# Moving the second attention's half steps, eighth by eighth, in between the column groups of the second block's projections

## The chip, the cores and the metric

The kernel runs on one core of one Trainium2 chip. The metric is the time of one execution on the device in microseconds (us); lower is better. The engines are named as the profile names them: PE is TensorE (PEld its weight loads), DVE is VectorE, ACT is ScalarE, POOL is GpSimd and SP is SyncE, which here only issues transfers.

## The reference: what is computed

512 tokens (x is 512 x 1024, float32) pass through two transformer blocks. The change touches the first half of the second block alone:

```python
h = rms_norm(x, norm_mix[l])
proj = h @ w_in[l]                       # 1024 x 2048
q, k, v, u = jnp.split(proj, [512, 1024, 1536], axis=-1)
a = moba_attention(q, k, v)              # 8 heads of 64
p = multiscale_pool(u, w_pool[l], pool_scale[l])
x = x + jnp.concatenate([a, p], axis=-1) @ w_out[l]
h = rms_norm(x, norm_mlp[l])
x = x + jnp.square(jax.nn.relu(h @ w_up[l])) @ w_down[l]
```

With 512 tokens and blocks of 256, every query attends to all tokens before it: `moba_attention` is causal softmax attention with an added bias of minus slope times distance, one slope for each head. `multiscale_pool` takes, for four groups of 128 channels of u, the mean over the last 2, 4, 8 or 16 tokens, subtracts the token, multiplies by a 128 x 128 matrix and scales each channel. The first block (its own attention beside a recurrence called rwkv7, then a feed-forward part) comes before it and is not changed.

## The kernel before

Everything is float32. Each large product is made of three products of rounded parts: an operand x is kept as `x_hi` (x rounded by a copy) and `x_lo` (x minus x_hi), and hi times hi, hi times lo and lo times hi are added up in PSUM. The 512 tokens are four row tiles (TT = 4) of 128 (P); the 1024 channels are eight tiles (KT = 8). Weights come in **groups** of 1024 x 256 (1 MB), numbered G_... through the whole program: SP loads group g into `w_raw[g % 2]`, ACT copies it to `w_hi[g % 2]` (`split` on ACT), DVE subtracts to get `w_lo[g % 2]` (`split` on DVE), and PE uses it. A group takes PE 48 matmuls of 512 columns or 96 of 256, and gives two PSUM tiles (T_... counts them; `mm_done` counts them finished, `tile_evacuated` counts them copied out; banks 0 to 3 rotate).

Every engine has its own program, written out by hand in order; engines wait for each other only through counted semaphores, and an engine does its instructions in the order of its text. So the order in the text is what sets the order of the work. The second block's mixing half stands thus on PE:

```python
first_tiles(N_MIX2, G_U2, T_U2)          # u: groups 49, 50
product_loop(G_QK2, T_QK2, 2)            # q, k: groups 51 to 54, channels on partitions (L404 to L406)
product_natural(G_V2, T_V2)              # v: groups 55, 56, tokens on partitions (L430 to L432)
```

then four small products of the pooled groups with `wpool` (L966, float32), then `attention(1)`, then the output product (L439 to L441) of groups 57 and 58 in `natural_group`, and of 59 and 60 in `out_pair`. Groups 61 and on are the feed-forward part.

`attention(b)` loops over four pairs of heads. A **half step** is one head and one tile of 128 queries, so there are 32. It is a chain over three engines: PE makes the scores (L912, of `qs` and the keys `ks0`, `ks1`, in which POOL has zeroed the other head's 64 channels, so that each product runs over 128 rows); DVE adds the bias (L1857) and takes the maximum (L1860, as a minimum of the negated scores); ACT takes the exponential with its sum (L1339); PE transposes (L919); ACT copies the transposes out (L1345); PE multiplies by the values (L928); DVE divides (L1844, L1846). After the four pairs PE transposes the result (L951), ACT and DVE make its hi and lo parts (L1350, L1425), and only then the output product can begin.

The first block's attention is built in another way: its half steps stand between steps of the recurrence, its scores (L779) use the 64 rows of the head alone, and bias and maximum are one DVE instruction (L1749) that writes over what it is to hold, with the exponential (L1257) in place. Its transposes are L788, the copies L1266, the products with the values L798.

DVE also makes the pooling windows (L1916 to L1924): before the first of them it takes the reciprocal of `rcnt` (L1911), 4 x 512 counts on each partition, which POOL has built (L2160, L2163).

## Time and profile before

| what | value |
|---|---|
| time before, median of 3 runs | 1400.87 us (1399.13 to 1403.6) |
| the profiled execution's own time | 1397.37 us |
| span of its trace | 1395.7 us |
| mean granted clock of TensorE | 0.982 |
| PE busy | 1304.2 us, 93% of the span |
| DVE busy | 635.5 us, 46% |
| ACT busy | 470.3 us, 34% |
| POOL busy | 250.8 us, 18% |

The profile is of one execution. An engine's busy time is the sum of its instructions; matmuls are pipelined and their ends are modelled, so the distance between the starts of two matmuls says more than the length of one. PEclk is the share of TensorE's full clock that was granted. The time outside the span is 1397.37 - 1395.7 = 1.7 us.

### The profile page before, as it was taken

How to read it: one execution, taken by the hardware profiler on the slowest of the kernel's cores; microseconds unless marked ns; L12 is line 12 of the kernel's file. 1: busy time of each engine (PE TensorE's matmuls, PEld its weight loads, DVE VectorE, ACT ScalarE, POOL GpSimd, SP SyncE). 2: the span in 40 equal slices, each digit the busy share in tenths (PEclk: the TensorE clock that was granted, in tenths of full speed). 3: DMA queues.
4: the chain of work that ended last, by engine and by line, in shares of the span. 5: the costliest groups of instructions: out<-in, count | busy, mean ns of one | idle time of the engine just before them, and what ended most of it. 6: DMA issues, size and time to landing. Idle time of an engine off the chain costs nothing.

```text
span 1395.7 us, 25137 instructions
## 1 busy us (share of the span) xinstructions
PE 1304.2 (93%) x10577; PEld 1163.4 (83%) x10577; DVE 635.5 (46%) x763; ACT 470.3 (34%) x758; POOL 250.8 (18%) x228
## 2 busy tenths in 40 slices
PE   5999989888799999999999887987999999999998
PEld 5677878777699889988899876865998899988998
DVE  5578635454347552134422646265255432245323
ACT  4446435335245222222222431266232211222222
POOL 6013325232102220012211030110003200022000
PEclk9999999999899999999999998998999999999999
DMA  5223100001052322223242122100313322222321
GB/s 181 75 61 120 61 2 3 2 3 50 14 182 75 107 91 95 90 91 104 72 151 92 61 68 91 61 1 19 118 61 104 106 91 91 90 90 90 106 92 61
DMA packets 99929, 108.95 MB, mean 78 GB/s; under 512 B 1907, under 2 KB 97189, under 8 KB 99845
## 3 DMA queue, kind: packets, MB, share of 16 engines
q1 hardware_dynamic: 99764, 107.45, 23.9%
q8 instruction: 67, 1.10, 0.3%
q0 software_dynamic: 80, 0.26, 0.1%
q14 instruction: 18, 0.14, 0.0%
HBM read 105.60 MB, written 2.10 MB: 77 GB/s over the span
## 4 chain that ended last, share of the span: by engine, by line
PE 78%; DVE 9%; issue 5%; ACT 4%; POOL 2%; DVEq 2%; POOLq 1%; ACTq 0%; DMA 0%
PE ps L404 11%; PE ps L406 11%; PE ps L405 11%; PE ps L439 10%; PE ps L440 10%; PE ps L441 10%; DVE w_lo L1420 2%; PE ps L490 1%; PE ps L491 1%; PE ps L492 1%; PE ps L432 1%; PE ps L430 1%; PE ps L431 1%; DVE rcnt L1911 1%; PE ps L668 1%
## 5 line engine op out<-in xcount | busy, mean ns | idle before, releaser
L1420 DVE TENSOR_TENSOR w_lo<-w_raw,w_hi 128x2048 fp32r<-128x2048 f32 (+1 forms) x93 | 212.1, 2280 | 241.4 <-ACT w_hi L985 238.2
L439 PE MATMUL ps<-w_hi,a_hi 128*128 128x256 f32 x1024 | 288.4, 282 | 0.9 <-DVE w_lo L1420 0.9
L440 PE MATMUL ps<-w_lo,a_hi 128*128 128x256 f32 x1024 | 288.0, 281 | 0.0
L441 PE MATMUL ps<-w_hi,a_lo 128*128 128x256 f32 x1024 | 288.0, 281 | 0.0
L404 PE MATMUL ps<-h_hi,w_hi 128*128 128x512 f32 x672 | 270.9, 403 | 13.1 <-DVE w_lo L1420 12.8
L406 PE MATMUL ps<-h_hi,w_lo 128*128 128x512 f32 x672 | 266.1, 396 | 0.0
L405 PE MATMUL ps<-h_lo,w_hi 128*128 128x512 f32 x672 | 266.0, 396 | 0.0
L985 ACT ACTIVATE w_hi<-w_raw 128x2048 fp32r<-128x2048 f32 (+1 forms) x90 | 171.2, 1903 | 162.8 <-PE ps L441 141.1
L2141 POOL TENSOR_TENSOR hsq<-tmp 128x512 f32<-128x512 f32 x64 | 103.3, 1616 | 568.3 <-ACT tmp L989 568.3
L439 PEld LDWEIGHTS ps<-w_hi,a_hi 128*128 128x128 f32 x1024 | 193.2, 189 | 1.5 <-DVE w_lo L1420 1.3
L440 PEld LDWEIGHTS ps<-w_lo,a_hi 128*128 128x128 f32 x1024 | 193.2, 189 | 0.2
L441 PEld LDWEIGHTS ps<-w_hi,a_lo 128*128 128x128 f32 x1024 | 193.2, 189 | 0.0
L404 PEld LDWEIGHTS ps<-h_hi,w_hi 128*128 128x128 f32 x672 | 126.5, 188 | 47.2 <-issue 14.8
L405 PEld LDWEIGHTS ps<-h_lo,w_hi 128*128 128x128 f32 x672 | 126.6, 188 | 32.4 <-issue 2.4
L406 PEld LDWEIGHTS ps<-h_hi,w_lo 128*128 128x128 f32 x672 | 126.4, 188 | 30.8
L1517 DVE TENSOR_TENSOR a_hi<-tmp 128x512 f32 (+1 forms) x64 | 47.5, 745 | 169.7 <-ACT tmp L989 169.7
L989 ACT ACTIVATE tmp<-ps 128x512 f32<-128x512 f32 x64 | 38.2, 598 | 248.8 <-PE ps L406 229.0
L439 PE MATMUL ps<-w_hi,h_hi 128*128 128x256 f32 x256 | 74.9, 292 | 11.3 <-DVE h_lo L1425 10.9
L490 PE MATMUL ps<-h_hi,w_hi 128*128 128x256 f32 x224 | 65.6, 293 | 12.2 <-DVE h_lo L1442 8.7
L440 PE MATMUL ps<-w_lo,h_hi 128*128 128x256 f32 x256 | 73.7, 288 | 0.0
L441 PE MATMUL ps<-w_hi,h_lo 128*128 128x256 f32 x256 | 73.6, 287 | 0.0
L491 PE MATMUL ps<-h_lo,w_hi 128*128 128x256 f32 x224 | 64.4, 288 | 0.0
(316 smaller groups left out, 1845.8 us busy)
## 6 DMA issues: line engine op xcount, KB each, us to landing
w_raw<-w_ffn_up_dram SPq DMA_DIRECT2D x16, 1024.0 KB, 5.3
w_raw<-w_ffn_down_dram SPq DMA_DIRECT2D x16, 1024.0 KB, 5.0
w_raw<-w_up_dram SPq DMA_DIRECT2D x16, 1024.0 KB, 5.3
w_raw<-w_down_dram SPq DMA_DIRECT2D x16, 1024.0 KB, 4.9
w_raw<-w_in_first_dram SPq DMA_DIRECT2D x12, 1024.0 KB, 5.3
w_raw<-w_out_dram SPq DMA_DIRECT2D x8, 1024.0 KB, 5.9
w_raw<-w_in_dram SPq DMA_DIRECT2D x8, 1024.0 KB, 5.3
xn<-x_dram SPq DMA_DIRECT2D x8, 512.0 KB, 6.5
```

Of the source, the lines that this page charges most:

```text
L404: mm(o, whi, hi[:, hb + k, :], start=first and k == 0, stop=False)
L405: mm(o, whi, lo[:, hb + k, :], start=False, stop=False)
L406: m = mm(o, wlo, hi[:, hb + k, :], start=False, stop=last and k == KT - 1)
L439: mm(o, hi[:, hb + k, tok], whi, start=first and own and k == ks[0], stop=False, skip_group_check=True)
L440: mm(o, hi[:, hb + k, tok], wlo, start=False, stop=False, skip_group_check=True)
L441: m = mm(o, lo[:, hb + k, tok], whi, start=False, stop=last and k == ks[-1], skip_group_check=True)
L490: mm(o[:, tok], whi, h_hi[:, k, tok], start=k == 0, stop=False)
L491: mm(o[:, tok], whi, h_lo[:, k, tok], start=False, stop=False)
L985: af(w_hi[:, g % 2, :, 0:n], w_raw[:, g % 2, :, 0:n], ACT.Copy).then_inc(sm["w_hi_ready"], 1)
L1420: v.tensor_tensor(w_lo[:, g % 2, :, 0:n], w_raw[:, g % 2, :, 0:n], w_hi[:, g % 2, :, 0:n].bitcast(F32), ALU.subtract).then_inc(sm["w_lo_re ...
L1517: v.tensor_tensor(a_hi[:, at_, :], tmp[:, m, :], tmp[:, m, :], ALU.mult)
L2141: g_.tensor_tensor(hsq[:, m % 2, :], tmp[:, m, :], tmp[:, m, :], ALU.mult)\
```

## The change

The second block's attention is rewritten after the manner of the first block's, and its half steps are put between eighths of the column groups. An eighth is an eighth of a group's matmuls: six of 512 columns or twelve of 256. After each comes a `tick`, and tick n holds the scores of half step n, the transposes of half step n - 2 and the products with the values of half step n - 3.

- **Order of the groups.** q and k of one pair of heads form one group (two transfers of 128 columns each), and the order is qk of pair 0, v of pairs 0 and 1, qk of pair 1, v of pairs 2 and 3, qk of pair 2, qk of pair 3 (`IN2`). Pairs 0, 1, 2 and 3 begin at ticks 0, 8, 24 and 32 (`PAIR_AT`); tick 0 is in the third group, ticks 32 to 47 are in the first two groups of the output product.
- **Attention.** Scores run over 64 rows; -1/8 is applied when q is copied out; POOL builds a table `bias` (eight multiplications of 128 x 512) in place of the staging of keys and queries; bias and minimum are one DVE instruction; `slopes`, `qs`, `ks0`, `ks1` go.
- **Pooling.** `rcnt` shrinks to 4 x 16 counts, the other tokens are multiplied by a constant; all four windows are made before DVE's third split; the small products stand after the first and the second group, and their results go to `m_hi` and `m_lo`.
- **Output product.** The groups are 512 rows by 512 columns (`mixed_step`): first the pooled rows, then the attention's. PE adds both into the same four PSUM tiles, DVE adds these to x at the end of the second group, and ACT then squares four pieces of 512 columns (before: eight of 256, four after each of the two groups).

The core of the diff:

```diff
-            product_loop(G_QK2, T_QK2, 2)
-            product_natural(G_V2, T_V2)
-            pe.wait_ge(sm["wpool_loaded"], 16)
-            for g in range(4):
...
-            attention(1)
-            pe.wait_ge(sm["hlo_ready"], H_OUT2 + 8)
-            for c in range(2):
-                natural_group(G_OUT2 + c, T_OUT2 + 2 * c, 0, h_hi, h_lo)
-            out_pair(N_FFN2, G_OUT2 + 2, T_OUT2 + 4)
+            in_and_attention()
+            last_pair(N_FFN2, G_OUT2 + 2, T_OUT2 + 4, mixed_rows)
```

```diff
+            def scores2(m):
+
+                p, t = m // 8, m // 2 % TT
+                pe.wait_ge(sm["max_ready"], 4 * H + m)
+                if m == 0:
+                    pe.wait_ge(sm["hlo_ready"], H_OUT2 + HP)
+                if t == 0:
+                    pe.wait_ge(sm["tile_evacuated"], T_IN2 + 2 * IN2.index(("qk", p)) + 2)
+                for e in range(2):
+                    mm(ps[:, 4 + e, 0:(t + 1) * P], qkT[half[e], p, t * P:(t + 1) * P], qkT[half[e], HP + p, 0:(t + 1) * P],
+                       start=True, stop=True).then_inc(sm["s_done"], 1)
...
+            def tick(n):
+
+                m = half_step(n)
+                if m is not None and m % 2 == 0:
+                    scores2(m)
+                m = half_step(n - 2)
+                if m is not None:
+                    turn_weights2(m)
+                m = half_step(n - 3)
+                if m is not None:
+                    values2(m)
+                if n in MIX_AT:
+                    turn_mix2(MIX_AT.index(n))
+
+            def pooled(g):
+
+                pe.wait_ge(sm["window_ready"], g + 1)
+                if g >= 2:
+                    pe.wait_ge(sm["hlo_ready"], H_OUT2 + g - 1)
...
+            def in_and_attention():
+
+                channels(0, None)
+                pe.wait_ge(sm["wpool_loaded"], 16)
+                pooled(0)
+                pooled(1)
+                tokens(1, None)
+                pooled(2)
+                pooled(3)
+                for n in range(2, 6):
+                    (channels if IN2[n][0] == "qk" else tokens)(n, 8 * (n - 2))
```

ACT's copies of the pooled products stand behind the copies of the second group (`mixed(1, j)`), and its last squares ahead of the split of group 60:

```diff
+            def in_and_attention():
+
+                split(G_IN2 + 1)
+                for j in range(2):
+                    mixed(0, j)
+                split(G_IN2 + 2)
+                for j in range(2):
+                    mixed(1, j)
+                for g in range(4):
+                    act.wait_ge(sm["pooled"], g + 1)
+                    af(m_hi[:, g, :], ps[:, 6 + g % 2, :], ACT.Copy, scale=cols("pool_scale_2", g)).then_inc(sm["hhi_ready"], 1)
...
+            in_and_attention()
+            act.wait_ge(sm["tile_evacuated"], T_OUT2 + 4)
+            for c in range(TT):
+                part(xn[:, c, 0:2 * GW], c, 0)
             split(G_OUT2 + 3)
```

POOL's table:

```diff
-            pool.wait_ge(sm["tile_evacuated"], T_V2)
-            clear_keys()
-            with pool.Fori(0, HP) as i:
-                stage_pair(i)
-                pool.wait_ge(sm["s_done"], at(8 * (HP + 1), i, 8))
+            for h in range(H):
+                m = g_.tensor_scalar(bias[:, h, :], delta[:, :], float(2.0 ** (-8.0 * (h + 1) / H)), None, ALU.mult)
+            m.then_inc(sm["bias_built"], 1)
```

How the instructions stand, read from the built programs. First PE, before, at the start of the second attention (L966 are the pooled products, `ks` the keys, `Pm` the exponentials, `PT` their transposes):

```order
L966 MATMUL ps<-uT,wpool 128x512 x4
L933 UNCONDITIONAL_BRANCH
L933 ISA
L912 MATMUL ps<-ks,qs 128x128
L912 MATMUL ps<-ks,qs 128x256
L912 MATMUL ps<-ks,qs 128x384
L917 ISA
L919 MATMUL ps<-ident,Pm 128x128
L912 MATMUL ps<-ks,qs 128x512
```

PE in the change, in the third group, from tick 1 to tick 3 (L1003 to L1005 are the projection; `tmp` now holds the exponentials and `hsq` their transposes):

```order
L1005 MATMUL ps<-h_hi,w_lo 128x512
L939 MATMUL ps<-qkT 128x256 x2
L948 MATMUL ps<-ident,tmp 128x128
L1003 MATMUL ps<-h_hi,w_hi 128x512
L1004 MATMUL ps<-h_lo,w_hi 128x512
L1005 MATMUL ps<-h_hi,w_lo 128x512
L1003 MATMUL ps<-h_hi,w_hi 128x512
L1004 MATMUL ps<-h_lo,w_hi 128x512
L1005 MATMUL ps<-h_hi,w_lo 128x512
L948 MATMUL ps<-ident,tmp 128x128
L959 MATMUL ps<-Vn,hsq 128x64
```

The attention's products, which stood together, now have six projection matmuls between one tick's and the next's.

DVE, in the change, behind the split of the second u group (L1567 is `split`, L2035 to L2046 are a window, `early` its first 16 tokens):

```order
L2091 RECIPROCAL rcnt<-rcnt 128x64
L2092 MEMSET upad 128x2x16
L2035 COPY upad<-uT 128x512
L2039 TENSOR_TENSOR upad<-upad 128x512
L2042 TENSOR_TENSOR early<-upad,rcnt 128x16
L2043 SCALAR_TENSOR_TENSOR uT<-upad,uT 128x496
L2046 TENSOR_TENSOR uT<-early,uT 128x16
L1567 TENSOR_TENSOR w_lo<-w_raw,w_hi 128x2048
L2035 COPY upad<-uT 128x512
L2039 TENSOR_TENSOR upad<-upad 128x512 x2
```

Before, the reciprocal was of 128x2048 and the split of group 52 stood right behind it, ahead of the first window; now the first window stands ahead of that split, and windows 1 to 3 ahead of the next.

ACT, in the change, at the end of the output product's second group (L1474 is the last hi part of the attention's result, L1104 the squares, L1095 `split`):

```order
L1474 ACTIVATE h_hi<-ps 128x512
L1104 ACTIVATE tmp,ssq<-xn 128x512
L1104 ACTIVATE hn_odd,ssq<-xn 128x512
L1104 ACTIVATE tmp,ssq<-xn 128x512
L1104 ACTIVATE hn_odd,ssq<-xn 128x512
L1095 ACTIVATE w_hi<-w_raw 128x2048
```

Before, only two squares of 128x256 stood between the last addition of that group and this split; now four of 128x512 do, and they wait for all four additions.

## Rows read from the trace of the kernel before

**Rows 1.** Windows: stretch, length, busy us of PE, PEld, DVE, ACT, POOL, PEclk, DMA.

```profile
821.70:833.00 11.30, 11.30 (x50) 8.86 (x48) 3.92 (x1) 3.00 (x3) 6.98 (x6) 1.00 0.31 93
833.00:844.40 11.40, 0.12 (x2) 0.03 (x1) 11.40 (x4) 2.40 (x2) 0.00 (x0) 0.69 0.00 0
844.40:902.20 57.80, 57.80 (x336) 50.87 (x337) 25.20 (x27) 12.61 (x13) 5.27 (x5) 0.97 0.29 91
902.20:907.00 4.80, 3.85 (x10) 1.18 (x8) 0.00 (x0) 3.54 (x6) 0.00 (x0) 1.00 0.00 0
907.00:963.40 56.40, 48.35 (x304) 36.82 (x304) 35.77 (x80) 37.07 (x100) 6.76 (x9) 1.00 0.00 0
...
973.30:998.00 24.70, 24.68 (x194) 24.68 (x195) 6.56 (x5) 5.59 (x14) 0.00 (x0) 0.92 0.47 150
```

**Rows 2.** Timeline of POOL, DVE and PE, 818 to 845: start, length, [idle before].

```profile
818.36 4.35 POOL L2160 CAST rcnt<-upad 128x512 f32<-128x512 int32 x4 [2.41 <-issue]
...
829.08 12.95 DVE L1911 RECIPROCAL rcnt<-rcnt 128x2048 f32<-128x2048 f32 x1 [7.96 <-POOL rcnt L2163]
...
844.37 0.79 PE L404 MATMUL ps<-h_hi,w_hi 128*128 128x512 f32 x1 [11.29 <-DVE w_lo L1420]
```

**Rows 3.** Timeline of PE inside the first block's attention.

```profile
188.78 0.49 PE L779 MATMUL ps<-qkT 64*128 64x128 f32 x4 [0.69 <-ACT Vn L1186]
189.21 0.56 PE L618 MATMUL ps<-krkv,bh 64*64 64x128 f32 x12
...
207.83 1.13 PE L779 MATMUL ps<-qkT 64*128 64x512 f32 x4
208.89 0.33 PE L788 MATMUL ps<-ident,Z 128*128 128x128 f32 x1
...
283.70 0.66 PE L788 MATMUL ps<-ident,Z 128*128 128x128 f32 x4
284.19 0.78 PE L798 MATMUL ps<-Vn,PT 128*128 128x64 f32 x6
284.90 0.28 PE L688 MATMUL ps<-hsq,Rm 64*64 64x64 f32 x2
```

**Rows 4.** Groups by line and form, 200 to 440: busy, mean ns | idle before.

```profile
L1257 ACT ACTIVATE Z<-Z,negmax 128x512 f32<-128x512 f32 x8 | 5.8, 724 | 7.4 <-DVE negmax L1749 7.4
L1749 DVE CUSTOM_DVE_ANT_0 Z<-lncount,ps 128x512 f32<-128x512 f32 x8 | 5.4, 672 | 2.0 <-PE ps L779 1.8 <-issue 0.2
```

**Rows 5.** Timeline of ACT at the end of the v groups.

```profile
902.41 0.60 ACT L1186 ACTIVATE Vn<-ps 128x512 f32<-128x512 f32 x1 [5.08 <-PE ps L432]
903.27 0.69 ACT L1389 ACTIVATE uT<-ps,par 128x512 f32<-128x512 f32 x1 [0.26 <-PE ps L966]
```

**Rows 6.** Timeline, POOL beside DVE in the second feed-forward part, and POOL's multiplications (L2163: ns min/median/max).

```profile
1047.99 2.89 POOL L2141 TENSOR_TENSOR hsq<-tmp 128x512 f32<-128x512 f32 x1 [1.36 <-ACT tmp L989]
...
1049.90 1.52 DVE L1517 TENSOR_TENSOR a_hi<-tmp 128x512 fp32r<-128x512 f32 x1
...
L2163 POOL TENSOR_SCALAR rcnt<-rcnt x4: 1481/1486/1517, 822.9 to 827.6; 128x512 f32<-128x512 f32 x4
```

**Rows 7.** Timeline around the split of group 60 and one square.

```profile
998.08 0.69 DVE L1530 TENSOR_TENSOR xn<-xn,ps 128x512 f32<-128x512 f32 x1 [4.75 <-PE ps L441]
...
999.87 1.90 ACT L985 ACTIVATE w_hi<-w_raw 128x2048 fp32r<-128x2048 f32 x1
...
1001.80 2.29 DVE L1420 TENSOR_TENSOR w_lo<-w_raw,w_hi 128x2048 fp32r<-128x2048 f32 x1 [3.03 <-ACT w_hi L985]
...
1004.15 0.39 PE L439 MATMUL ps<-w_hi,h_hi 128*128 128x256 f32 x1 [0.43 <-DVE w_lo L1420]
...
1022.00 0.63 ACT L994 ACTIVATE tmp<-xn 128x512 f32<-128x512 f32 x1 [3.24 <-DVE xn L1945]
```

**Rows 8.** A pause of PE and the window right behind it.

```profile
795.40 0.36 PE L490 MATMUL ps<-h_hi,w_hi 128*128 128x256 f32 x1 [3.40 <-DVE h_lo L1442]
...
795.40:799.40 4.00, 4.00 (x22) 4.00 (x23) 1.94 (x5) 2.97 (x7) 0.00 (x0) 0.62 0.00 0
```

More of the change, by code:

```diff
@@ L88, in program @@
         rstd = sb("rstd", [P, S])
-        slopes = sb("slopes", [P, 2, HP, 2])
         delta = sb("delta", [P, S])
@@ new lines, in pooled, with channels @@
+            def pooled(g):
+                pe.wait_ge(sm["window_ready"], g + 1)
+                if g >= 2:
+                    pe.wait_ge(sm["hlo_ready"], H_OUT2 + g - 1)
+                mm(ps[:, 6 + g % 2, :], wpool[:, g, :], uT[:, g, :], start=True, stop=True).then_inc(sm["pooled"], 1)
+            def channels(n, base):
+                g, tile = G_IN2 + n, T_IN2 + 2 * n
+                pe.wait_ge(sm["w_lo_ready"], g + 1)
+                for j in range(2):
+                    pe.wait_ge(sm["tile_evacuated"], tile + j - 3)
+                    o = ps[:, (tile + j) % 4, :]
+                    for k in range(KT):
+                        whi, wlo = (w[:, g % 2, k, j * P:(j + 1) * P] for w in (w_hi, w_lo))
+                        mm(o, whi, h_hi[:, k, :], start=k == 0, stop=False)
+                        mm(o, whi, h_lo[:, k, :], start=False, stop=False)
+                        m = mm(o, wlo, h_hi[:, k, :], start=False, stop=k == KT - 1)
+                        if k == KT - 1:
+                            m.then_inc(sm["mm_done"], 1)
+                        if base is not None and k % 2:
+                            tick(base + 4 * j + k // 2)
@@ new lines, in tokens @@
+            def tokens(n, base):
+                g, tile = G_IN2 + n, T_IN2 + 2 * n
+                pe.wait_ge(sm["w_lo_ready"], g + 1)
+                for c in range(TT):
+                    if c % 2 == 0:
+                        pe.wait_ge(sm["tile_evacuated"], tile + c // 2 - 3)
+                    for k in (0, 4):
+                        m = row_product(ps[:, (tile + c // 2) % 4, c % 2 * GW:(c % 2 + 1) * GW], rows(c), g, 0, h_hi, h_lo, k == 0, k == 4,
+                                        own=c % 2 == 0, ks=range(k, k + 4))
+                        if c % 2 and k:
+                            m.then_inc(sm["mm_done"], 1)
+                        if base is not None:
+                            tick(base + 2 * c + k // 4)
@@ new lines, in mixed_step, with mixed_rows @@
+            def mixed_step(o, c, g, hi, lo, k, first, last):
+                whi, wlo = wide(w_hi, g)[:, k, :], wide(w_lo, g)[:, k, :]
+                mm(o, hi[:, k, rows(c)], whi, start=first, stop=False)
+                mm(o, hi[:, k, rows(c)], wlo, start=False, stop=False)
+                return mm(o, lo[:, k, rows(c)], whi, start=False, stop=last)
+            def mixed_rows(c, late):
+                g = G_OUT2 + 2 + late
+                for k in range(HP):
+                    m = mixed_step(ps[:, (T_OUT2 + 4 + c) % 4, :], c, g, *((m_hi, m_lo), (h_hi, h_lo))[late], k,
+                                   late == 0 and k == 0, late == 1 and k == HP - 1)
+                return m
@@ L1171, in _ @@
                         norm_root(p)
-            def qk(g, tile):
-                with act.Fori(0, 2) as i:
-                    for c in range(2):
-                        split(g + c + 1, i, 2)
-                        for j in range(2):
-                            m = 2 * c + j
-                            evacuate(g + c, j, tile + m, qkT[:, i * 4 + m, :], i, 2)
             def natural_v(g, tile):
```

395 lines of the change are left out of this document (224 added, 171 removed).

## The prediction

> **What bounds the kernel now.** I read first the busy shares, then the windows by stage. PE is busy for 93% of the span (the table above), and the stages around the change show where the rest is lost. [rows 1] cut the stretch from the first matmul of group 51 (821.7) to the last of group 58 (998.0), 176.3 us, into its parts. The reader is to see three things in them. Where PE only projects (844.4 to 902.2), it never stops, at a clock of 0.97: 57.8 x 0.97 / 5 = 11.2 us for a group. Behind the first group PE does nothing for 11.4 us. And in the second attention (907.0 to 963.4, 56.4 us) PE shows 48.35 us of busy time, DVE 35.8 and ACT 37.1: three engines that pass small pieces to each other, none of them full. Behind it come 9.9 us more until the output product starts (963.4 to 973.3), and that starts at a low clock (0.92 over 24.7 us, so 24.7 x 0.08 = 2.0 us lost).
>
> The timeline names the cause of the 11.4 us: PE waits 11.29 us for `w_lo` of group 52, whose split stands on DVE behind the reciprocal of `rcnt`, 12.95 us for 2048 counts, and that waited 7.96 us for POOL to build them [rows 2].
>
> So the bound in this stretch is not an engine but order. What the change can win is the 176.3 us less PE's own work, if the work of the other engines fits beside it.
>
> **PE's own work in the change.** Eight groups (six of the projection, two of the output product) at 11.2 us: 89.6 us. A half group of 512 x 512 is the same 48 matmuls of 512 columns. The four pooled products stay: 3.85 us [rows 1].
>
> The attention's products are priced by the first block's, which is built in the same way [rows 3], from start to next start, since lengths overlap. Scores of both heads: 189.21 - 188.78 = 0.43 us at 128 columns, 208.89 - 207.83 = 1.06 at 512; between them in proportion, so 0.43 + 0.64 + 0.85 + 1.06 = 2.98 for a pair, 11.9 for four. Transposes: 284.19 - 283.70 = 0.49 for four, 80 of them 9.8 us. Values: 284.90 - 284.19 = 0.71 for six records, 0.118 each; 80 products of two records, 18.9 us. Transposing the result, 16 at 0.1225: 2.0 us. Together 42.6 us.
>
> Sum of PE's work: 89.6 + 3.85 + 42.6 = 136.0 us.
>
> **Does the rest fit beside it?** A tick takes PE 11.2 / 8 = 1.4 us of projection and on average 42.6 / 32 = 1.3 us of attention. From the scores of a half step to its transposes lie two ticks, about 5.4 us. In them DVE's bias and minimum take at most 0.67 us and ACT's exponential 0.72 [rows 4], with the scores some 2.5 us. In one tick of eight a split of 1.90 stands ahead on ACT and one of 2.29 on DVE [rows 7]; 2.5 + 1.9 = 4.4 still fits, and DVE's split falls in the tick without scores. So I cost the 32 half steps at nothing beyond PE's own work; what hides them is the six matmuls of 512 columns between two ticks. Without that cover a half step costs what it does now, 56.4 / 32 = 1.76 us, 0.43 more than 1.33.
>
> The transfers: q and k come in two pieces of 128 columns, 512 bytes in a row for 1 KB before. Group 53's is issued when `w_lo` of group 51 is done, 821, and ACT wants it at 833. The trace has no such transfer; from nothing more to twice the time of now, which lands as in 10 us, it is covered. The gain row's load moves behind the last transposes of the attention and is wanted some 25 us later. Nothing for both.
>
> Four waits on PE are left, and I walk through them.
>
> - *The third pooled product* waits until `m_lo` of the first is made. ACT makes `m_hi` only behind its copies of the second group, so from that group's end: a copy 0.60, `m_hi` 0.69 [rows 5], `m_lo` on DVE about 0.69 (the addition out of PSUM of the same size [rows 7]) and three hand-overs of about 0.1: **2.4 us**.
> - *Tick 0* waits for all four `m_lo`: one more `m_hi` and `m_lo` behind the fourth product, 1.5 us against 1.4 of projection, with hand-overs **0.4 us**.
> - *Edges of pairs and the last hi and lo parts*: scores of pairs 1 and 3 wait for a copy (2.1 us against 2.0 of cover), the last eighths for `h_lo` of pair 3 (transposes, copy, subtraction, about 1.7 behind 1.4): **0.6 us** in all.
> - *The second pooled product* waits for window 1 on DVE. POOL's counts are now tiny; they are ready about 3 us after its 818.36 [rows 2]. From 821.4 DVE has a small reciprocal, window 0 (2.4 us with its drains), the split of group 52 (2.3) and window 1 (3.2, operations of 0.69), so it would be done at about 829.8, and PE wants it at 834.1. But beside it POOL now does eight multiplications of 1.49 us [rows 6], to about 834.
>
> **A place where POOL and DVE meet.** The trace shows this meeting in the feed-forward part: a POOL operation issued into a DVE split takes 2.89 us, and the DVE operation behind it 1.52 [rows 6], where one of 128x512 takes 0.69 [rows 7]. So a DVE operation on SBUF beside POOL costs up to 0.83 us more. Window 0 and window 1 hold seven large ones; with all of them delayed window 1 ends 5.8 us later, at 835.6, and if the small ones and the copies are delayed as well, at about 838. Bounds for PE's wait are 0 and 4 us, from these rows; I take **2 us**.
>
> The Trainium skill (SBUF — State Buffer, section "SBUF: two separate sides") says that GpSimd and a VectorE operation with two SBUF inputs share a port pair as an exclusive lock, and that the loser blocks for the whole instruction. The trace agrees that both are delayed (2.89 and 1.52 us), but the DVE operation lost only part of POOL's. By the rule taken strictly the sum would be 5.6 us larger before any clock; by the rows it is the 2 us above. It is the second rival below.
>
> Sum of the stretch: 136.0 + 2.4 + 0.4 + 0.6 + 2 = 141.4 us, against 176.3: **34.9 us less**.
>
> **What is late next.** Group 60's weights. Before, its split on ACT stood behind one addition and two squares of 256 columns: addition 998.08 to 998.77, squares until 999.87, ACT's split, DVE's split until 1004.1, and PE could go on at 1004.15, 6.15 us behind the group's end [rows 7], having waited 0.43. In the change ACT waits for all four additions (the last two behind the end: 1.5 us) and makes four squares of 0.63 us with a read of the sum, about 0.8 each (two of half the width took 1.1): 3.2 us. Then 1.90 and 2.29 for the splits: 1.5 + 3.2 + 1.9 + 2.3 + 0.3 = 9.2 us behind the end. PE has 5.6 us of work there (the two first row tiles), so it stops for about 3.6 us. Cost against before: 9.2 - 6.15 = **3.1 us**. A pause of that size (3.40 us) was followed by a window of 4 us at a granted clock of 0.62 on average [rows 8], most of it at the lower of the two levels, 1.2 GHz: 4 x 0.38 = **1.5 us** more. Its bounds are 0 (if the clock stays) and 3.
>
> Net: 34.9 - 3.1 - 1.5 = 30.3 us. The profiled execution took 1397.4, so the changed kernel would take 1367.1 in it. The median of the three runs lies 3.5 us above that execution, so in its terms 1400.9 - 30.3 = 1370.6: I say **1371 us**, a ratio of 0.979.
>
> **The rivals.**
>
> 1. *As forecast*, 1362 to 1377. The lower end is without the meeting with POOL, without the low clock, and with half of the other waits (30.3 + 2 + 1.5 + 1.7 = 35.5, so 1365), and 3 us for what runs scatter.
> 2. *POOL and DVE exclude each other fully.* Then DVE's 8.4 us of work and POOL's 8 x 1.49 = 11.9 us stand in line: 821.4 + 20.3 = 841.7, and PE waits 7.6 us at the second pooled product in place of 2, with another 1.5 us at the low clock: 1371 + 7.1 = 1378. For it: the 2.89 us. Against it: 1.52 is less than 0.69 + 1.49.
> 3. *The cover is not used.* Each half step costs 1.76 us as now, on top of the eighths, since an engine's order makes its neighbours wait: 32 x 0.43 = 14 us, 1385. Against it: the first block's half steps, which stand between steps of the recurrence in the same way, and whose scores followed without a pause in one of the two places shown and after 0.69 us in the other [rows 3].
> 4. *Slower than before.* The same place with a higher price: PE, which keeps its order, waits at every tick for a chain that is longer than two ticks. From 30.3 / 32 = 0.95 us a half step the gain is gone, and at 1.3 us the kernel takes 1371 + 42 = 1413. It would take a chain of some 2 x 2.7 + 1.3 = 6.7 us against the 2.5 to 4.4 counted above. Little speaks for it.
> 5. *No difference*: 3 with twice its price, 1399.
>
> **How the numbers follow.** The three runs lie 0.3% apart, so 0.3% (4 us) is about what can be told from no change. Chances: 1 has 0.72, 2 has 0.12, 3 has 0.07, 5 has 0.03, 4 has 0.06. Faster by over 0.3% are 1 to 3: 0.91; the same 0.03; slower 0.06. The range reaches from the lower end of the first case, 1362, to the third, 1386; it leaves out 4, 5 and the edges, about 0.15.
>
> **What the profile after would show.** PE: no pause of 11 us ahead of the second group; a pause of 0 to 4 us at the second pooled product and 2.4 at the third; from tick 0 to tick 47 a busy PE at the full clock with no wait of over 0.5 us; a pause of 3 to 4 us ahead of the late half of the last pair of groups, for `w_lo`. From the first matmul of group 51 to the last of group 58: 138 to 146 us. DVE: additions near 0.7 us stretched to 1.5 beside POOL's table. It would be wrong if PE's waits at the ticks add up to more than 5 us, if scores, transposes and values take more than 42.6 us between float32r matmuls (the switch between the two kinds in this mix is in no row), or if the clock falls inside the ticks.

## The result, and the profile after

The changed kernel takes **1364.01 us** (median of four runs, 1361.7 to 1365.47); the kernel before took 1400.82 beside it. The ratio is 0.974, with an interval of 0.9722 to 0.9759: 36.8 us faster. The profiled execution took 1362.8 us, its span is 1361.1 (before 1397.37 and 1395.7), and the mean granted clock is 0.984.

The first part of the page, busy time by engine, after:

```profile
PE 1289.9 (95%) x10385; PEld 1141.6 (84%) x10385; DVE 605.7 (45%) x759; ACT 460.4 (34%) x741; POOL 245.7 (18%) x213
```

The windows of the changed kernel: the first matmul of group 51 to the last of group 58; of this, from tick 0 on; from the end of group 58 to the late half of the last pair of groups; that half; and everything from the feed-forward part on. Columns as in [rows 1].

```profile
820.80:960.26 139.46, 136.43 (x810) 109.10 (x809) 57.72 (x118) 60.03 (x128) 14.50 (x11) 1.00 0.24 72
...
850.76:960.26 109.50, 108.83 (x650) 86.35 (x651) 35.31 (x84) 50.03 (x117) 0.00 (x0) 1.00 0.20 63
...
960.26:969.16 8.90, 5.77 (x26) 4.32 (x24) 3.72 (x5) 4.70 (x9) 0.00 (x0) 0.98 0.01 2
...
969.16:991.60 22.44, 20.18 (x88) 16.16 (x89) 10.64 (x16) 8.20 (x15) 0.00 (x0) 0.93 0.29 94
...
991.61:1361.10 369.49, 362.74 (x2416) 331.57 (x2416) 144.18 (x131) 88.89 (x106) 51.63 (x32) 0.99 0.28 90
```

The stretch that took 176.3 us takes 139.46. Half steps and projection together keep PE at a clock of 1.00 for 109.5 us and show 108.8 of them busy, where the half steps by themselves took 56.4 us with 48.35 busy and 11.4 us went by in which PE did nothing [rows 1].

These are all of PE's pauses of more than 0.15 us between 780 and 1005, from its timeline (the idle time before an instruction, and what ended it, stand in brackets):

```profile
794.35 0.36 PE L512 MATMUL ps<-h_hi,w_hi 128*128 128x256 f32 x1 [3.43 <-DVE h_lo L1589]
...
847.19 1.96 PE L992 MATMUL ps<-uT,wpool 128*128 128x512 f32 x4 [2.14 <-DVE m_lo L2102]
...
850.76 0.49 PE L939 MATMUL ps<-qkT 64*128 64x128 f32 x4 [0.22 <-issue]
...
933.65 0.43 PE L959 MATMUL ps<-Vn,hsq 128*128 128x64 f32 x2 [0.65 <-DVE On L2007]
...
969.16 0.79 PE L1029 MATMUL ps<-w_hi,h_hi 128*128 128x512 f32 x1 [3.13 <-DVE w_lo L1567]
...
991.61 0.36 PE L512 MATMUL ps<-h_hi,w_hi 128*128 128x256 f32 x1 [2.27 <-DVE h_lo L1589]
```

The first and the last of them were there before (3.40 at 795.40, and 2.19 at 1025.4, ahead of the feed-forward part). I call what lies between those two **the stage**; it is what all runs below are compared by, since what lies ahead of it scatters by some us from one execution to the next. It took 1025.4 - 795.4 = 230.0 us before and takes 991.61 - 794.35 = 197.26 now: 32.7 us less. The other 1.9 us of the 34.6 between the two spans lie outside: 1.05 ahead of the stage, in text that is the same in both, and 0.8 behind it (370.3 against 369.5).

### The profile page after: what moved, and what is told of

Same layout as the page of the kernel before. It is cut to its first block, busy times and chain, and to the rows that moved or that the text cites. A ratio compares the mean times of both kernels' runs of the same rounds, so it can differ in the third digit from the quotient of the medians.

```text
span 1361.1 us, 24506 instructions
## 1 busy us (share of the span) xinstructions
PE 1289.9 (95%) x10385; PEld 1141.6 (84%) x10385; DVE 605.7 (45%) x759; ACT 460.4 (34%) x741; POOL 245.7 (18%) x213
## 4 chain that ended last, share of the span: by engine, by line
PE 82%; DVE 7%; issue 4%; ACT 4%; POOL 1%; DVEq 1%; ACTq 0%; POOLq 0%; DMA 0%
PE ps L426 10%; PE ps L428 10%; PE ps L427 10%; PE ps L461 9%; PE ps L462 9%; PE ps L463 9%; DVE w_lo L1567 2%; PE ps L512 2%; PE ps L514 1%; PE ps L513 1%; PE ps L1003 1%; PE ps L1004 1%; PE ps L1005 1%; PE ps L959 1%; PE ps L690 1%
## 5 line engine op out<-in xcount | busy, mean ns | idle before, releaser
L1567 DVE TENSOR_TENSOR w_lo<-w_raw,w_hi 128x2048 fp32r<-128x2048 f32 (+1 forms) x93 | 212.2, 2282 | 227.2 <-ACT w_hi L1095 224.3
L426 PE MATMUL ps<-h_hi,w_hi 128*128 128x512 f32 x608 | 244.8, 403 | 1.8 <-DVE w_lo L1567 1.2
L428 PE MATMUL ps<-h_hi,w_lo 128*128 128x512 f32 x608 | 240.5, 395 | 0.0
L427 PE MATMUL ps<-h_lo,w_hi 128*128 128x512 f32 x608 | 240.4, 395 | 0.0
L1095 ACT ACTIVATE w_hi<-w_raw 128x2048 fp32r<-128x2048 f32 (+1 forms) x90 | 171.3, 1903 | 160.1 <-PE ps L463 138.6
L426 PEld LDWEIGHTS ps<-h_hi,w_hi 128*128 128x128 f32 x608 | 114.2, 188 | 32.3 <-issue 3.1
L427 PEld LDWEIGHTS ps<-h_lo,w_hi 128*128 128x128 f32 x608 | 114.2, 188 | 29.3 <-issue 2.4
L428 PEld LDWEIGHTS ps<-h_hi,w_lo 128*128 128x128 f32 x608 | 114.2, 188 | 27.7
L514 PE MATMUL ps<-h_hi,w_lo 128*128 128x256 f32 x224 | 65.0, 290 | 0.0
L461 PE MATMUL ps<-w_hi,h_hi 128*128 128x256 f32 x192 | 56.8, 296 | 5.4 <-DVE h_lo L1572 5.4
L1670 DVE TENSOR_TENSOR a_lo<-hsq,a_hi 128x512 f32 (+1 forms) x64 | 57.1, 930 | 7.1 <-issue 6.8
```

The lines of the kernel that those rows point to most:

```text
L426: mm(o, whi, hi[:, hb + k, :], start=first and k == 0, stop=False)
L427: mm(o, whi, lo[:, hb + k, :], start=False, stop=False)
L428: m = mm(o, wlo, hi[:, hb + k, :], start=False, stop=last and k == KT - 1)
L461: mm(o, hi[:, hb + k, tok], whi, start=first and own and k == ks[0], stop=False, skip_group_check=True)
L514: m = mm(o[:, tok], wlo, h_hi[:, k, tok], start=False, stop=k == KT - 1)
L1095: af(w_hi[:, g % 2, :, 0:n], w_raw[:, g % 2, :, 0:n], ACT.Copy).then_inc(sm["w_hi_ready"], 1)
```

## The experiments

### The counts alone

The kernel before, with nothing changed but `rcnt`: 4 x 16 counts, the other tokens multiplied by a constant (DVE's part is shown; POOL builds the fewer counts). Attention and order stay.

```diff
-                v.tensor_tensor(upad[:, (g + 1) % 2, 16:16 + S], upad[:, (g + 1) % 2, 16:16 + S], rcnt[:, g, :], ALU.mult)
-                dve.drain()
-                v.tensor_tensor(uT[:, g, :], upad[:, (g + 1) % 2, 16:16 + S], uT[:, g, :], ALU.subtract)\
-                    .then_inc(sm["window_ready"], 1)
+                total = upad[:, (g + 1) % 2, 16:16 + S]
+                v.tensor_tensor(early[:, :], total[:, 0:16], rcnt[:, g, :], ALU.mult)
+                v.scalar_tensor_tensor(out=uT[:, g, 16:S], in0=total[:, 16:S], scalar=2.0 ** -(g + 1), in1=uT[:, g, 16:S],
+                                       op0=ALU.mult, op1=ALU.subtract)
+                dve.drain()
+                v.tensor_tensor(uT[:, g, 0:16], early[:, :], uT[:, g, 0:16], ALU.subtract).then_inc(sm["window_ready"], 1)
```

> The kernel before, with one part of the change alone: 16 counts for each window in place of 512, and a constant for the other tokens. My account: the pause of 11.3 us ahead of the second q and k group goes, and with it the low clock behind it (about 1.7 us), nothing new is late, since the split would be done some 6 us before PE wants it: 1400.8 - 13 = 1388 us, ratio 0.991. Rival A (the pause is worth more, since windows and splits on DVE stand in each other's way all along): 1380 or less. Rival B (something else holds the group, such as ACT's half of the split): 1400, no change.

Measured: 1385.65 us (1383.53 to 1386.95), ratio 0.9902 (0.9881 to 0.9923). The stage takes 216.34 us, 13.7 less than before. The pause of 11.29 us is gone, and the others stay, the longest of them behind the attention:

```profile
950.20 3.72 PE L953 MATMUL ps<-ident,On 128*128 128x128 f32 x16 [1.20 <-DVEq L1867]
...
959.43 0.58 PE L441 MATMUL ps<-w_hi,h_hi 128*128 128x256 f32 x1 [5.51 <-DVE h_lo L1427]
```

So 13.7 of the 32.7 us come from an edit that has nothing to do with where the half steps stand. They are the pause of 11.29, the clock behind it (0.97 over 57.8 us [rows 1], 1.00 here: 1.7 us), and 0.8 us in the attention, where three of PE's waits for the exponentials are shorter (0.87, 0.86 and 0.86 us for 1.12, 1.12 and 1.10).

### The half steps in a row

The changed kernel, with ticks 0 to 31 in one row behind the last projection group, on PE, ACT and DVE (shown for PE). These ticks hold the 24 half steps of pairs 0, 1 and 2; pair 3 stays between the eighths of the output product.

```diff
                 for n in range(2, 6):
-                    (channels if IN2[n][0] == "qk" else tokens)(n, 8 * (n - 2))
+                    (channels if IN2[n][0] == "qk" else tokens)(n, None)
+                for n in range(32):
+                    tick(n)
```

> The changed kernel with ticks 0 to 31 (24 half steps, pairs 0 to 2) in one row behind the last projection group, on PE, ACT and DVE alike; pair 3 stays between the eighths of the output product. Splits and copies of the groups stand without ticks between them. My account: a half step in a row costs 1.76 us as in the kernel before, 0.43 more than PE's own work: 24 x 0.43 = 10 us more than the changed kernel's 1364.0, so 1374, with waits of PE for the exponentials and the copies in every tick. Rival A (the new form of the half step is what was won, and the order is worth nothing): 1364 to 1366. Rival B (a tick is a chain of scores, bias, exponential, transposes, copy and values with little in flight, 2.5 us and more): 24 x 1.2 = 29 us more, 1393.

Measured: 1388.05 us (1385.6 to 1393.64), ratio 0.9929. It is 24.0 us slower than the changed kernel, and the stage takes 222.8 us, 25.5 more. PE's timeline where the row begins:

```profile
893.82 0.70 PE L939 MATMUL ps<-qkT 64*128 64x256 f32 x4 [0.70 <-DVE negmax L1998]
...
895.20 0.33 PE L948 MATMUL ps<-ident,tmp 128*128 128x128 f32 x1 [0.67 <-ACT tmp L1447]
...
895.98 0.45 PE L948 MATMUL ps<-ident,tmp 128*128 128x128 f32 x1 [0.46 <-ACT hsq L1455]
```

and the windows of what follows:

```profile
895.80:923.00 27.20, 25.68 (x98) 18.28 (x99) 5.55 (x22) 11.06 (x36) 0.00 (x0) 0.50 0.00 1
...
923.00:945.00 22.00, 19.44 (x103) 14.80 (x104) 5.81 (x22) 11.55 (x32) 0.00 (x0) 0.73 0.00 1
```

I had expected waits, of one size or another. PE's waits come to some 6 us in all. Most of the rest is the clock: at the third of three small waits it falls to 0.50, the lower of its two levels (1.2 GHz), and stays there for 27.2 us, though PE is shown busy for 25.7 of them; later it falls once more. 27.2 x 0.50 + 22 x 0.27 = 19.5 us, which is a rough figure, since a few of PE's waits fall in these windows too. No term of mine had this, and the busy share can't show it, since a matmul at half the clock is busy for longer (the scores of 384 keys 1.65 us here, 0.92 in the rows of eight below). The kernel before had its half steps in a row too, and kept 1.00 [rows 1]. What was different is tried next.

### The row again, with scores over all 128 rows

The kernel of the last experiment, with the scores written as the kernel before had them as far as PE is concerned: over 128 rows. It leaves out what keeps the heads apart: each score is the sum over both heads of the pair. The size of the work is that of the kernel before.

```diff
-                    mm(ps[:, 4 + e, 0:(t + 1) * P], qkT[half[e], p, t * P:(t + 1) * P], qkT[half[e], HP + p, 0:(t + 1) * P],
+                    mm(ps[:, 4 + e, 0:(t + 1) * P], qkT[:, p, t * P:(t + 1) * P], qkT[:, HP + p, 0:(t + 1) * P],
```

> The half steps of ticks 0 to 31 in one row, and the scores over all 128 rows (they become the sum over both heads of a pair). The run with the row and 64-row scores took 1388.05 us, and its clock fell to 0.55 in the row, although PE is shown busy for 26.84 us of 30. Theory A: the clock fell because the 64-row scores (and the thin mix around them) use less of the array than the 128-row scores of the kernel before, whose own row of half steps kept 1.00. Then with 128-row scores the clock stays at 1.00 in the row: 1388.0 - 19.4 (30 x 0.45 and 22 x 0.27) + 3.0 (what the wider scores cost) = about 1372 us, and the stage from the pause ahead of the second block's first projection to the one ahead of its feed-forward part is 206 us in place of 222.8. Theory B: the rows have nothing to do with it, the row's small waits and hand-overs do. Then the clock falls again and it takes 1388 to 1392 us. I give A 0.4.

Measured: 1372.29 us (1371.47 to 1376.85), ratio 0.9817 (0.9791 to 0.9842): 15.8 us **faster** than the row with the cheaper scores. The window of the row:

```profile
893.00:945.00 52.00, 45.08 (x275) 35.77 (x275) 19.02 (x65) 31.47 (x89) 0.00 (x0) 1.00 0.05 13
```

The clock stays at 1.00. The waits are much like those of the 64-row version (0.39, 0.28 and 0.16 again and again; 6.9 us of idle time in the whole row), except at the start of the row, where they are 0.48, 0.43 and 0.46 for 0.70, 0.67 and 0.46. The wider scores put more rows to work, keep PE at them for longer and shorten these first waits; which of the three decides isn't told apart here.

### The same wide scores in the changed kernel

The same line, in the changed kernel, with its ticks between eighths; here too each score is the sum over both heads.

> The changed kernel; the scores run over all 128 rows of q and k of the pair, in place of the 64 rows of the head, so both heads' scores become the sum over both heads: that part of the computation is changed. Everything else is as before. My account: products over the upper and the lower 64 rows overlap on PE (2.98 us a pair for both heads); over 128 rows they stand in line, by the second attention of the kernel before 0.22, 0.43, 0.65 and 0.87 us each, so 4.34 us a pair: 5.4 us more, 1369.4. Rival (the rows make no difference, only the columns do): 1364.0.

Measured: 1366.97 us (1364.14 to 1370.75), ratio 0.9763. The medians lie 3.0 us apart and the runs overlap, so the stage has to tell: it takes 200.47 us, 3.2 more than in the changed kernel where 5.4 were expected. The timelines, first of the changed kernel, then of this one, at a half step of 512 keys:

```profile
862.78 0.40 PE L1005 MATMUL ps<-h_hi,w_lo 128*128 128x512 f32 x1
863.11 1.13 PE L939 MATMUL ps<-qkT 64*128 64x512 f32 x4
864.16 0.55 PE L948 MATMUL ps<-ident,tmp 128*128 128x128 f32 x3
864.55 0.56 PE L959 MATMUL ps<-Vn,hsq 128*128 128x64 f32 x4
```

```profile
867.58 0.40 PE L1005 MATMUL ps<-h_hi,w_lo 128*128 128x512 f32 x1
867.82 1.88 PE L939 MATMUL ps<-qkT 128*128 128x512 f32 x4
869.53 0.49 PE L948 MATMUL ps<-ident,tmp 128*128 128x128 f32 x3
869.86 0.33 PE L959 MATMUL ps<-Vn,hsq 128*128 128x64 f32 x2
```

From start to start the scores take 1.05 us against 1.71. But ahead of the 64-row ones 0.33 us lie between the last projection matmul's start and theirs, and 0.24 ahead of the 128-row ones; and the three transposes behind them take 0.39 to the next start against 0.33. So the two changes between 64 and 128 rows cost 0.09 and 0.06 us here. Sixteen times 0.15 is 2.4 us (an estimate from this one half step), which brings the 5.4 us near the 3.2 measured.

With this run there is a ladder of stages in which the clock keeps up in the half steps: 230.0 before; 216.34 with the small counts (-13.7); 209.28 with the rewritten attention, order and output product, 24 of the half steps in a row (-7.1, which no run takes apart further); 200.47 with these 24 between eighths (-8.8); 197.26 with 64-row scores (-3.2).

### Four rows of eight, and ticks in twos

Ticks 0 to 31 in four rows of eight, each behind a whole group; and, in another kernel, two ticks behind each quarter of a group. Both are shown for PE, the second for the groups with channels on partitions; the other groups alike. The third of the four rows (ticks 16 to 23) starts no half step and only finishes those of pair 1.

```diff
                 for n in range(2, 6):
-                    (channels if IN2[n][0] == "qk" else tokens)(n, 8 * (n - 2))
+                    (channels if IN2[n][0] == "qk" else tokens)(n, None)
+                    for i in range(8):
+                        tick(8 * (n - 2) + i)
```

```diff
-                        if base is not None and k % 2:
-                            tick(base + 4 * j + k // 2)
+                        if base is not None and k % 4 == 3:
+                            tick(base + 4 * j + k // 2 - 1)
+                            tick(base + 4 * j + k // 2)
```

> Ticks 0 to 31 in four rows of eight, each behind a whole projection group, in place of one row of 32 behind all of them. Theory A: the waits of a row are paid (PE's idle in the row of 32 adds up to about 6 us, of which 5 more than in the changed kernel, and each of some 15 hand-overs costs about 0.2 us beyond the idle shown, since the last matmul's tail no longer overlaps: 8 us in all), and a row of 10 us is too short for the clock to fall, or it falls once: 1364 + 8 = 1372 us, up to 1376. Theory B: the clock falls in each of the four rows as it did in the long one, for most of 10 us: 8 + 4 x 5 = 28 us more, 1392 us.

> The changed kernel; PE does two ticks together behind each quarter of a group in place of one behind each eighth; ACT and DVE are not changed. My account: from the scores of a half step to its transposes there is still a quarter of a group (2.8 us) and a tick, about 4.1 us, against a chain of 2.5; only where a split stands ahead (4.4) is there a short wait, at most 0.3 us six times: 1364 to 1366. Rival A (the eighths' cover is needed in full): 32 x 0.43 = 14 us more, 1378. Rival B (the fine change between the two kinds of matmul costs PE time in itself): 2 us or more less.

Measured, rows of eight: 1370.22 us (1368.31 to 1372.18), ratio 0.9788, stage 204.04. The clock stays at 1.00 in all four rows. The first of them begins as the row of 32 does, with the same products and the same waits:

```profile
863.92 0.70 PE L939 MATMUL ps<-qkT 64*128 64x256 f32 x4 [0.70 <-DVE negmax L1998]
...
865.29 0.33 PE L948 MATMUL ps<-ident,tmp 128*128 128x128 f32 x1 [0.67 <-ACT tmp L1447]
...
866.08 0.30 PE L948 MATMUL ps<-ident,tmp 128*128 128x128 f32 x1 [0.46 <-ACT hsq L1455]
```

In the row of 32 the clock was falling at this very place, 3 us into the row:

```profile
895.00:895.50 0.50, 0.30 (x1) 0.14 (x1) 0.33 (x2) 0.50 (x4) 0.00 (x0) 1.00 0.00 0
895.50:896.00 0.50, 0.04 (x2) 0.05 (x1) 0.00 (x0) 0.47 (x3) 0.00 (x0) 0.74 0.00 0
```

So the first fall can't be put down to the 64-row scores with these three waits, which the first row of eight had too, nor to the length of the row, most of which was still to come. What was different up to there is what PE had done before the row (four projection groups without a tick, against one) and the moment at which it came. It isn't a freak of one execution: the mean clocks of the four runs are 0.966 to 0.973 with the row of 32, 0.985 to 0.989 with wide scores, 0.984 to 0.989 in rows of eight.

In twos: 1374.68 us (1372.73 to 1377.54), ratio 0.9829, stage 206.97, 9.7 more than in the changed kernel, where I had expected at most 2. Two stretches of PE in twos:

```profile
856.04 0.33 PE L948 MATMUL ps<-ident,tmp 128*128 128x128 f32 x1
856.83 0.30 PE L948 MATMUL ps<-ident,tmp 128*128 128x128 f32 x1 [0.46 <-ACT hsq L1457]
...
940.92 0.43 PE L959 MATMUL ps<-Vn,hsq 128*128 128x64 f32 x2 [1.81 <-DVE On L2011]
...
968.55 0.50 PE L1031 MATMUL ps<-w_hi,h_hi 128*128 128x512 f32 x1 [1.41 <-DVE h_lo L2019]
```

I had counted the chain from scores to transposes. Two others bite. All transposes go into one bank, so those of the second tick wait until ACT has copied out those of the first (0.46, 0.40, 0.28 and 0.16 us for one to four of them, 4.1 us in thirteen waits). And the first values of a pair wait for DVE's division of the pair before (0.95 and 1.81 us), the output product for the last `h_lo` (1.41): 4.2 us in three waits. The idle shown is not all of it either: from start to start the first pair takes 0.79 us, where transposes that follow each other take 0.11, so 0.68 is lost for 0.46 shown. Behind the wait of 1.81 us the clock falls as well:

```profile
941.16:945.00 3.84, 3.84 (x12) 3.03 (x12) 0.69 (x1) 0.29 (x1) 0.00 (x0) 0.56 0.68 263
```

That is 3.84 x 0.44 = 1.7 us. The low clock in the late half of the last pair of groups is absent in this execution (21.08 us for 22.44: 1.4 less). Waits add up to 7.4 us more than in the changed kernel, so 9.7 - 7.4 - 1.7 + 1.4 = 2.0 us are left. They are what sixteen waits cost beyond the idle shown, less what is saved by changing half as often between half steps and projection; no run tells the two apart.

### The last split ahead of the squares

```diff
-            act.wait_ge(sm["tile_evacuated"], T_OUT2 + 4)
-            for c in range(TT):
-                part(xn[:, c, 0:2 * GW], c, 0)
             split(G_OUT2 + 3)
+            act.wait_ge(sm["tile_evacuated"], T_OUT2 + 4)
+            for c in range(TT):
+                part(xn[:, c, 0:2 * GW], c, 0)
```

> The changed kernel; ACT does its half of the split of group 60 ahead of the wait for the four additions and the four squares, not behind them. My account: the pause of 3.13 us ahead of the late half goes wholly (the split would be done 4.5 us behind the group's end, PE has work for 5.6 us), and the low clock behind it too (1.7 us): 1364.0 - 4.8 = 1359.2. Rival A (the low clock does not hang on this pause but comes anyway): 1360.9. Rival B (the squares are now late, and the sum of squares for the next norm with them): 1363 to 1365, with a longer pause where the norm's rows are waited for.

Measured: **1354.87 us** (1354.78 to 1355.58), ratio 0.9681 (0.9664 to 0.9698); the stage takes 192.59 us, 4.7 less than in the changed kernel. ACT and DVE at that place in the changed kernel:

```profile
961.84 0.63 ACT L1104 ACTIVATE tmp<-xn 128x512 f32<-128x512 f32 x1 [5.26 <-DVE xn L2113]
962.38 0.19 ACT L1104 ACTIVATION_READ_ACCUMULATOR tmp<-xn 128x1 f32 x1
...
964.88 1.90 ACT L1095 ACTIVATE w_hi<-w_raw 128x2048 fp32r<-128x2048 f32 x1
...
966.81 2.29 DVE L1567 TENSOR_TENSOR w_lo<-w_raw,w_hi 128x2048 fp32r<-128x2048 f32 x1 [5.06 <-ACT w_hi L1095]
```

and ACT with the split first:

```profile
958.65 1.92 ACT L1095 ACTIVATE w_hi<-w_raw 128x2048 fp32r<-128x2048 f32 x1 [3.93 <-PE ps L1031]
960.64 0.63 ACT L1104 ACTIVATE tmp<-xn 128x512 f32<-128x512 f32 x1
```

The split needs the buffer that PE gives back at 958.65, and neither the additions nor the squares; and the sum that DVE makes of the squares (ready at 964.22) is read only at 969.92. PE's pause of 3.13 us is gone, and the granted clock from 960 to 984.9 is 1.00 where it was 0.93. The medians lie 9.1 us apart. Outside the stage the two traces differ by 2.0 us ahead of it and by 1.6 behind it, where the clock this time stayed up after the pause of 2.31 us (1.00 over the next 8 us, 0.79 in the changed kernel).

### The first `m_hi` ahead of the last copies

```diff
-                for j in range(2):
-                    mixed(1, j)
                 for g in range(4):
+                    if g == 2:
+                        for j in range(2):
+                            mixed(1, j)
                     act.wait_ge(sm["pooled"], g + 1)
```

> The changed kernel; ACT makes the hi parts of the first two pooled products ahead of its copies of the second group's tiles, not behind them. My account: the pause of 2.14 us at the third pooled product goes and the 0.2 us at tick 0 stays or goes: 1364.0 - 2.2 = 1361.8, a difference at the edge of what the runs can tell, but the trace must show no pause there. Rival (DVE, which has the windows and a split to do, is what holds the third product): the pause stays above 1 us.

Measured: 1359.56 us (1357.99 to 1365.51), ratio 0.972 (0.9696 to 0.9745). The pause of 2.14 us ahead of the third pooled product is gone; the stage takes 193.5 us, 3.7 less, of which 1.4 is the low clock behind the 3.13 us pause, absent in this execution (21.08 us for 22.44).

### All three

Both edits, and the hi and lo parts of pairs 0 and 1 at ticks 36 and 38 in place of 33 and 35, so that none of them stands on DVE ahead of pair 2's division, which is in tick 35 (the third edit is shown for ACT; DVE's is the same).

```diff
-                if n in (33, 35):
-                    p = (n - 33) // 2
+                if n in (36, 38):
+                    p = (n - 36) // 2
```

> The changed kernel with three moves: ACT's split of group 60 ahead of the squares, the first two pooled hi parts ahead of the second group's copies, and the hi and lo parts of the attention's pairs 0 and 1 made at ticks 36 and 38 in place of 33 and 35 (so that DVE reaches pair 2's division sooner, for which PE waited 0.65 us). My account: the pauses of 3.13, 2.14 and 0.65 us and a low clock of 1.7 go: 1364.0 - 7.6 = 1356.4. Rival (a pause that goes is given back at the next wait, since the norm behind the output product is bound by DVE and ACT): 1360 to 1362.

Measured: **1353.76 us** (1351.53 to 1357.26), ratio 0.9672 (0.9657 to 0.9688), the fastest here. The stage takes 189.2 us, 8.1 less than in the changed kernel where 7.6 were expected. All pauses of PE of over 0.15 us that are left between 800 and 1000:

```profile
851.18 0.49 PE L939 MATMUL ps<-qkT 64*128 64x128 f32 x4 [0.20 <-issue]
...
986.35 0.36 PE L512 MATMUL ps<-h_hi,w_hi 128*128 128x256 f32 x1 [2.28 <-DVE h_lo L1590]
```

The median is only 1.1 us below that of the split alone, within what the runs scatter: of the two, only the stages (189.2 and 192.59) tell that the other edits do anything.

### POOL's table later

POOL waits for the fourth window before it builds the bias table.

```diff
+            pool.wait_ge(sm["window_ready"], 4)
             for h in range(H):
                 m = g_.tensor_scalar(bias[:, h, :], delta[:, :], float(2.0 ** (-8.0 * (h + 1) / H)), None, ALU.mult)
```

> The changed kernel; POOL builds the table of biases only when all four windows are made. This is to show what the meeting of POOL and DVE costs. My account: DVE's split beside POOL goes from 2.64 to 2.29 us, the copy from 0.83 to 0.43, the windows are made some 2 us sooner; PE did not wait for them, so nothing is won, and the table is ready at about 852, up to 1 us behind the first half step: 1364 to 1365. Rival (these lengths have another cause, such as the small operations ahead): the lengths stay.

Measured: 1361.87 us (1361.04 to 1363.56), ratio 0.9736 (0.9722 to 0.9751), the same as the changed kernel; the stage takes 197.21 against 197.26. DVE behind window 0 with POOL's table beside it, and PE's first two pooled products, in the changed kernel's timeline; then DVE without the table:

```profile
821.55 10.77 POOL L2326 TENSOR_SCALAR bias<-delta 128x512 f32<-128x512 f32 x6
...
824.79 2.64 DVE L1567 TENSOR_TENSOR w_lo<-w_raw,w_hi 128x2048 fp32r<-128x2048 f32 x1
827.36 0.83 DVE L2035 COPY upad<-uT 128x512 f32<-128x512 f32 x1
828.26 1.74 DVE L2039 TENSOR_TENSOR upad<-upad 128x512 f32<-128x512 f32 x2
...
830.91 0.42 DVE L2046 TENSOR_TENSOR uT<-early,uT 128x16 f32<-128x16 f32 x1
...
831.97 1.88 PE L992 MATMUL ps<-uT,wpool 128*128 128x512 f32 x4
```

```profile
823.34 2.29 DVE L1567 TENSOR_TENSOR w_lo<-w_raw,w_hi 128x2048 fp32r<-128x2048 f32 x1
825.55 0.42 DVE L2035 COPY upad<-uT 128x512 f32<-128x512 f32 x1
826.04 1.46 DVE L2039 TENSOR_TENSOR upad<-upad 128x512 f32<-128x512 f32 x2
```

The meeting is there: the split costs 0.35 us more beside POOL, the copy 0.41, two additions 0.28. Window 0, from 822.17 on and beside POOL too, has its copy, addition and long subtraction at the lengths that they have without the table (0.43, 0.69 and 0.67). But window 1 is ready at 831.33, and PE comes to the first of the two products at 831.97 and to the second, which needs window 1, behind it. So it is hidden, with 0.64 us and a product to spare.

The Trainium skill's rule of an exclusive lock, which blocks the loser for the whole instruction (SBUF — State Buffer, section "SBUF: two separate sides"), is not what these rows show: POOL multiplies from 821.55 without a gap, so a DVE held out for a whole instruction would have lost up to 1.49 us [rows 6] at each operation, and it lost 0.41 at most.

## Why the prediction was right, and where its sizes were off

Predicted: 1371 us. Measured: 1364.01, inside the range near its lower end. The mechanism is the forecast's, case 1: the pause of 11.29 us and the chain of the half steps are gone from PE's time, and the waits that were foreseen, but for one, are there. Where the 7 us come from:

- **The stretch from group 51 to group 58**: predicted 141.4, measured 139.46, 1.9 less. Three of its waits came as worked out: 2.14 us at the third pooled product (2.4), 0.22 at tick 0 (0.4), 0.65 at an edge (0.6). The edge is another one than those named, though: PE waits there for DVE's division of pair 2, and neither for a copy of scores nor for the last `h_lo`. The fourth, for window 1, was put at 2 us and is **nil**: this is the term that was mis-sized. Seven large operations were to lose 0.83 us each; the two windows hold five, and two copies, and beside POOL's table they lost between nothing and 0.41, the split 0.35. Window 1 was ready before PE wanted it. Rival 2, full exclusion, falls with it, and moving the table away changed nothing. The waits are 2.4 us less than forecast and the stretch only 1.9: PE's own work is 0.5 more.
- **The attention's own work**: 109.50 us from tick 0 on, less 5.875 groups of 11.2, less the 0.65 of waits that fall in it, leaves 43.0 us, against 42.6. That the sum comes so near is in part luck. It left out what changing costs: 0.15 us at the rows of each score, as the run with wide scores shows, and 0.08 behind each tick, whose first projection matmul takes 0.32 us to the next start (864.91 to 865.23) where the others take 0.23 or 0.24. And it put a record of the values at 0.118 us where it takes 0.09 (864.55 to 864.91 for four).
- **The half steps cost nothing beyond PE's own work**: true, and the runs show what the cover is worth. In a row at the full clock it is 8.8 us of the stage for 24 half steps, 0.37 each, near the 0.43 of rival 3. With the new 64-row scores the row cost 25.5 us, 1.06 each, three quarters of it clock. "Without that cover a half step costs what it does now" holds for the waits and fails for the clock, which the old form had kept in its row.
- **Group 60's weights**: 9.2 us behind the group's end was predicted and 8.9 measured, with a pause of 3.13 for 3.6. The low clock behind it came as taken, 22.44 x 0.07 = 1.6 us for 1.5; that it came was luck as far as the runs tell, for in three of the eight kernels with this pause it didn't. The window from the group's end to the feed-forward part is 31.35 us against 27.4: 3.95 for 4.6. Undoing the order alone gave back 4.7.
- **Outside the stage** 1.9 us, in text that the change doesn't touch, and 2.3 us from the step from the profiled execution to the median: it lay 3.5 us below the median before, and only 1.2 after. The prediction carried the 3.5 over. These 4.2 us of the 7 are scatter between executions and say nothing about the mechanism.

Together: 1.9 + 0.65 - 0.15 (ahead of the stretch) + 1.9 + 2.3 = 6.6 of the 7 us; the rest is rounding.

Of the three things that were to prove it wrong, two did not come in the changed kernel: PE's waits at the ticks add up to 0.87 us, and the clock is 1.00 in the ticks. The second, more than 42.6 us for the attention's products, came by 0.4 us: the changes between the two kinds of matmul do cost something, and values cheaper than their price hide most of it. The third came in the row of 32. Why the clock falls there isn't settled: it stayed up in the runs with wide scores and in those with rows of eight, and what these have in common isn't known.

## What to carry to other kernels

Look at what holds the long pauses before crediting the big rewrite: here a reciprocal over 2048 counts that were needed for 16 tokens each was 13.7 of 32.7 us in the stage. When small chained steps are cut into a large product, one at a time with the product's matmuls between is what pays; in twos they wait on each other through the bank that they share, and on the division between two pairs. And after such a change read which instruction the *next* product's operands stand behind: one split moved ahead of four squares that nobody wanted yet was worth 4.7 us more of the stage.

## What the runs showed of the hardware that I had not expected

- A row of half steps with 64-row scores had its clock at 0.50 for 27.2 us with PE shown busy for 25.7; with 128-row scores and nearly the same waits it had 1.00 over 52 us and the kernel was 15.8 us faster for doing more work. Cut into four rows of eight, the 64-row version kept 1.00 too, though its first row begins with the very waits (0.70, 0.67, 0.46 us) at which the clock of the long row fell.
- A pause of some 3 us is not followed by a low clock each time: behind the pause of 3.13 or 3.14 us ahead of group 60's late half the clock over that half was 0.93 in the changed kernel, with the table later and with wide scores, 0.92 in the row with wide scores and 0.87 in the row with 64-row ones, and 1.00 with the `m_hi` edit, in the rows of eight and in twos. Each is one trace of another kernel, so whether one kernel would show both isn't shown. A shorter pause can be followed by one: behind 1.81 us it was 0.56 over 3.84 us, in twos.
- A wait inside a chain of small matmuls costs more than the idle time shown: 0.68 us for 0.46, read from start to start at one of them.
- The changes between matmuls of 128 rows and scores of 64 cost 0.09 us going in and 0.06 coming out, read at one half step.
- Operations of DVE beside a busy POOL ran as long as without it or up to twice as long (0.69 for 0.69 us, 2.64 for 2.29, 0.83 for 0.42), and were not held out for the whole of POOL's instructions, which themselves took 1.78 us (14.20 for eight) for 1.49 [rows 6].
